# New orders of issue in a four-mixer block kernel: opening loads, mLSTM heads with a mask table, input blocks, merges and boundaries turned by pairs

## What is computed

```python
h = x
u = rmsnorm(h, norm_mix[0]); h = h + mlstm_mixer(u, ...)     # stage A: 4 heads, 128 wide keys, 256 wide values
h = h + swiglu(rmsnorm(h, norm_ffn[0]), w_in[0], w_out[0])   # hidden width 2816
u = rmsnorm(h, norm_mix[1]); h = h + moba_mixer(u, ...)      # stage B: 8 heads of 128
h = h + swiglu(rmsnorm(h, norm_ffn[1]), w_in[1], w_out[1])
# stage C, the second network's block
p = rms_norm(h, norm1) @ w_in_2                              # window attention, hyena, differential attention, 3 gates
a = window_attention(...)        # 8 query heads of 64, masked to a distance of 128
b = hyena_branch(...)            # short convolution, two long convolutions by spectra of generated filters, gates
c = diff_attention(...)          # 4 heads, two softmaxes subtracted, then an rms norm
merged = sigmoid(g0) * (a @ w_oa) + sigmoid(g1) * (b @ w_ob) + sigmoid(g2) * (c @ w_oc)
h = h + merged @ w_out_2
out = h + swiglu(rms_norm(h, norm2), ...)
```

## Time and profile before

| | us |
|---|---|
| median of 3 runs | 1113.66 |
| lowest, highest | 1113.09, 1119.86 |
| profiled execution, its own time | 1115.49 |
| its span, first to last instruction | 1113.7 |
| TensorE busy in it | 1072.1 |
| VectorE, ScalarE busy | 722.5, 539.7 |

### The profile page before, as it was taken

The page is one execution under the profiler, slowest core; times in us unless marked ns, Lnnn a source line. Parts: engine busy times, 40 slices in busy tenths (PEclk is TensorE's granted clock), DMA queues, the critical chain, the costliest instruction groups (busy, mean ns, idle before and its releaser), DMA issues.

```text
span 1113.7 us, 14635 instructions
## 1 busy us (share of the span) xinstructions
PE 1072.1 (96%) x4942; PEld 865.8 (78%) x4942; DVE 722.5 (65%) x1209; ACT 539.7 (48%) x828; POOL 40.0 (4%) x48
## 2 busy tenths in 40 slices
PE   5999999999999999999999999899999999999998
PEld 3777678888887778788888878676777777888887
DVE  2865876555557987754554579787868666555553
ACT  3564355443444546643443464446456445443442
POOL 5003000000000200000000000000000000000000
PEclk9999999999999999999999999999999999999999
DMA  9464256655565544566555553543444355655553
GB/s 256 123 169 132 77 153 193 191 188 183 189 189 170 169 151 126 158 189 186 189 188 181 179 170 97 168 132 114 136 146 133 118 182 163 190 188 182 189 188 112
DMA packets 133598, 182.04 MB, mean 163 GB/s; under 512 B 11446, under 2 KB 80322, under 8 KB 133490
## 3 DMA queue, kind: packets, MB, share of 16 engines
q1 hardware_dynamic: 132266, 178.40, 50.9%
q0 software_dynamic: 1056, 2.57, 1.1%
q10 hardware_dynamic: 232, 0.49, 0.1%
HBM read 180.36 MB, written 1.05 MB: 163 GB/s over the span
## 4 chain that ended last, share of the span: by engine, by line
PE 76%; DVE 14%; ACT 5%; issue 2%; DMA 1%; SPq 1%; POOL 0%; DVEq 0%; ACTq 0%; POOLq 0%
PE ps L1802 15%; PE ps L1813 14%; PE ps L1805 14%; PE ps L1823 7%; PE ps L1824 7%; PE ps L1828 7%; DVE wlo L998 4%; PE ps L1787 2%; PE ps L1789 2%; PE ps L1788 2%; PE ps L1893 1%; DMA raw<-in_a_w_in 1%; ACT whi L537 1%; PE ps L1876 1%; PE ps L2015 1%
## 5 line engine op out<-in xcount | busy, mean ns | idle before, releaser
L998 DVE TENSOR_TENSOR wlo<-raw,whi 128x1024 fp32r<-128x1024 f32 x338 | 406.6, 1234 | 145.3 <-ACT whi L537 144.7
L537 ACT ACTIVATE whi<-raw 128x1024 fp32r<-128x1024 f32 x338 | 342.3, 1052 | 117.7 <-DMA raw<-in_ffn_w 27.6
L1802 PE MATMUL ps<-whi,ath 128*128 128x512 f32 (+1 forms) x896 | 359.3, 402 | 8.3 <-DVE atl L1012 4.3
L1805 PE MATMUL ps<-whi,atl 128*128 128x512 f32 (+1 forms) x896 | 351.4, 393 | 0.0
L1813 PE MATMUL ps<-wlo,ath 128*128 128x512 f32 (+1 forms) x896 | 241.4, 391 | 3.3 <-DVE wlo L998 3.3
L1802 PEld LDWEIGHTS ps<-whi,ath 128*128 128x128 f32 x896 | 169.6, 189 | 52.6 <-issue 12.0
L1813 PEld LDWEIGHTS ps<-wlo,ath 128*128 128x128 f32 x896 | 168.0, 189 | 40.3 <-DVE wlo L998 5.3
L1805 PEld LDWEIGHTS ps<-whi,atl 128*128 128x128 f32 x896 | 169.8, 189 | 33.3 <-issue 0.5
L1823 PE MATMUL ps<-whi,brh 128*128 128x512 f32 x272 | 106.5, 392 | 0.4 <-issue 0.4
L1824 PE MATMUL ps<-whi,brl 128*128 128x512 f32 x272 | 105.9, 389 | 0.0
L1074 DVE TENSOR_TENSOR brl<-ps,brh 128x512 fp32r<-128x512 f32 x33 | 22.8, 692 | 94.6 <-ACT brh L583 94.6
(11 more groups left out here) (339 smaller groups left out, 1006.5 us busy)
## 6 DMA issues: line engine op xcount, KB each, us to landing
raw<-in_ffn_w_in SPq DMA_DIRECT2D x176, 256.0 KB, 2.9
raw<-in_ffn_w SPq DMA_DIRECT2D x132, 256.0 KB, 2.9
raw<-in_w_in SPq DMA_DIRECT2D x104, 256.0 KB, 2.9
raw<-in_ffn_w_out SPq DMA_DIRECT2D x88, 256.0 KB, 2.8
raw<-in_a_w_in SPq DMA_DIRECT2D x48, 256.0 KB, 3.3
raw<-in_b_w_in SPq DMA_DIRECT2D x48, 256.0 KB, 3.0
raw<-in_a_w_out SPq DMA_DIRECT2D x16, 256.0 KB, 2.8
raw<-in_b_w_out SPq DMA_DIRECT2D x16, 256.0 KB, 2.8
```

The costliest lines, as they stand in the source:

```text
L537: a_(unit_view(whi, slot, w), unit_view(raw, slot, w), ACT.Copy).then_inc(hi_ready, 1)
L998: v_.tensor_tensor(unit_view(wlo, slot, w), unit_view(raw, slot, w), unit_view(whi, slot, w), ALU.subtract).then_inc(lo_ready, 1)
L1802: mm(ps[bk + t][:, 0:w], ath[:, k, t * P:(t + 1) * P], rh[:, kk, :], start=k == 0, stop=False)
L1805: mm(ps[bk + t][:, 0:w], atl[:, k, t * P:(t + 1) * P], rh[:, kk, :], start=False, stop=False)
```

## The change

No arithmetic changes but the mask of stage A: a table `maskA` of 128x256 (large values above the diagonal, then zeros) takes the place of the constant 0.0 in `a_dist`'s max, so that exp gives zero there, and GpSimd's `affine_select` goes. The rest moves instructions.

```diff
 # opening, SyncE: x first, unit 0, small rows, units on
-nc.sync.dma_start(con[:, 0:P], D["consts"][:, 0:P])
-sp.wait_ge(sem("cleared"), 1)
-nc.sync.dma_start(grow[0:mix.shape[0], :], mix)
 for t in range(NT):
     nc.sync.dma_start(x[:, t, :], xv[:, t, :])
+load_in(U_A, D["a_w_in"][0], 0)
+sp.wait_ge(sem("cleared"), 2)
 for name, src, w in rows: ...
-for i in range(6):
+for i in range(1, 6):
     load_in(U_A + 4 * i, D["a_w_in"][0], 512 * i)
 # GpSimd: the two small filter weights first, then in steps
+nc.gpsimd.dma_start(fw12[0:33, 0, :], ...)
+nc.gpsimd.dma_start(fw12[:, 1, :], ...)
+pool.wait_ge(raw_loaded[0], 32)
 nc.gpsimd.dma_start(wg[:, :, :], ...)
 ... # the twelve parameters
+pool.wait_ge(raw_loaded[1], 64)
+pool.wait_ge(sem("filt_loaded"), 32)
 nc.gpsimd.dma_start(A_dec, D["decay"])
 nc.gpsimd.dma_start(work[0:64, 18968:18968 + 2048], D["filt_w3_2"][0])
-for h in range(AH):
-    pool.wait_ge(sem("a_p_ready"), h + 1)
-    ... nc.gpsimd.affine_select(out=blk, in_=blk, ...)
 # ScalarE
-nc.scalar.dma_start(con[:, P:N_FIRST], ...)
+nc.scalar.dma_start(con[:, 0:P], ...)
+nc.scalar.dma_start(grow[0:mix.shape[0], :], mix)
+turn_hi(0, mix_gain, (0,))
 feed(1)
-turn_hi(0, ...)
+nc.scalar.dma_start(con[:, P:N_FIRST], ...)
+turn_hi(0, mix_gain, (1, 2, 3))
 # TensorE: five products of zeros, x turned tile by tile of tokens, the small rows' transpose and
 # the filter product behind block 0 and in block 1
+pe.wait_ge(sem("cleared"), 1)
+for _ in range(5):
+    mm(ps[7][:, 0:S], hid[:, 0, 0:P], hid[:, 0, :], start=True, stop=True)
-turn(lambda t: x[:, t, :], x_first)
+for t in range(NT):
+    pe.wait_ge(sem(f"x_loaded{t}"), 16)
+    for p in range(4): ... transposes of tile t
+units(0, use=0)
 nc.tensor.transpose(ps[7][:, 256:384], grow[:, :], ident)
-units(0, use=0)
-units(1, beside=gate_products)
+units(1, 0, 2, beside=gate_products)
+mm(ps[7][0:64, 0:S], fw12[0:33, 0, :], ...)
+units(1, 2, 4, beside=gate_products)
 # stage A's heads
-feed(24 + AHEAD)                      # ScalarE and VectorE, ahead of the heads
+dve.wait_ge(sem("con2_loaded"), 64)
-v_.tensor_scalar(A_D[...], mb[:, 0:S], am[:, 0, h:h + 1], 0.0, ALU.subtract, ALU.max)
+v_.scalar_tensor_tensor(A_D[...], mb[:, 0:S], am[:, 0, h:h + 1], maskA, ALU.subtract, ALU.max)
-pe.wait_ge(sem("a_p_masked"), 2 * h + 2)
+pe.wait_ge(sem("a_p_ready"), h + 1)
+evac(5, ...)                          # now ahead of a_weights(2)
-norm_sum(1)                           # VectorE: now behind turn_lo(1, (0, 1)) and spectrum(2)
 # boundaries, five places
-down_end(end, ..., at=(1, 1), between=lambda: x_turn(r + 1, (0, 1)))
+down_end(end, ..., between={(1, 0): turn pair 0, (1, 1): turn pair 1})
 # stage C: window blocks ahead of the hyena's third part
-C_COLS = ((768, 512), (1280, 512), (1792, 512), (0, 512), (512, 256), (2304, 512), ...)
+C_COLS = ((768, 512), (1280, 512), (0, 512), (512, 256), (1792, 512), (2304, 512), ...)
 # TensorE
-units(15, 0, 1); backward(0); units(15, 1, 3); h_back(1); units(15, 3, 4); forward(1); units(16)
+units(15, 0, 2); backward(0); units(15, 2, 4); units(16, 0, 1); h_back(1); units(16, 1, 2); forward(1); units(16, 2, 4)
 # VectorE, behind hyena_gate(0)
-feed(20); spectral(1); feed(21); spectral_imag(1); feed(22); spectral_end(1); feed(24)
-c_sums x3; h_taps(2); feed(26); c_norms; rotations of both token tiles
+feed(18); c_sums x3; c_norms; c_rotate(0, 0, 8, 0, None)
+feed(20); spectral(1); feed(22); spectral_imag(1); feed(24); spectral_end(1); feed(25); h_taps(2); feed(26)
+the other rotations
 # ScalarE, ahead of the window heads
+a_(sm[:, 126:127], con[:, 0:1], ACT.Exp)          # ahead of the wait for c_w_turned
-act.wait_ge(sem("h_z"), 4); a_(obh[...], h_v, ACT.Copy)   # now behind w_exp(0) and its splits
+w_exp(0) ahead of feed(W_STEPS[0]); c_squares of C_pd behind w_pt(0)
 # VectorE: w_logits(0) ahead of feed(U_C + 32), w_prob(0) behind it
 # differential heads and merges
-feed(D_STEPS[0]); merge(0, ...)
+feed(U_GC + 2); merge(0, ...); feed(D_STEPS[0])
-d_exp(2) whole; gate_evac(24, 0)
+d_exp(2, comp 0); gate_evac(24, 0); d_exp(2, comp 1)
+down_unit(U_OB, ...)                  # TensorE: ahead of d_pv(3)
-one rsqrt and scaling for four heads; feed(U_OC + 2) ahead of c_hi and c_lo
+d_norms(0), d_norms(1) by two heads, each with its own transposes; feed(U_OC + 3) ahead of c_hi and c_lo
-merge(1, both halves); feed(U_W + 2); merge(2, half 0); turn_lo(6, (0, 1)); merge(2, half 1)
+merge(1, half 0); merge(1, half 1, tile 0); merge(2, half 0); feed(U_W + 2); turn_lo(6, (0, 1))
+feed(U_W + 3); merge(1, half 1, tile 1); merge(2, half 1)
-mg_turn((0, 1)) at (3, 0) of the U_OC down_end; down_unit(U_W); mg_turn((2, 3)); units 1 to 5 of U_W
+mg_turn((0, 1)) at (2, 1); down_end of units 0 to 2 of U_W; mg_turn((2, 3)); units 3 to 5
```

More of the change, by code:

```diff
@@ L104 @@
 _at = 0
-for _name, _n in (("ident", P), ("ones", P), ("sel", AH * P), ("zT", S), ("nrmw", 4), ("inv", BROT // 2),
+for _name, _n in (("ident", P), ("ones", P), ("sel", AH * P), ("zT", S), ("nrmw", 4), ("inv", BROT // 2), ("maskA", S),
                   ("cosC", NT * HD // 2), ("sinC", NT * HD // 2), ("maskB", 384), ("maskW", NT * S),
@@ L799, in h_evac @@
             def h_evac(c):
-                evac(12 + c, lambda t: C_ph[:, c, t, :], n=4, tiles=(0, 1))
+                evac(H_BLOCKS[c], lambda t: C_ph[:, c, t, :], n=4, tiles=(0, 1))
             def h_conv(c):
@@ L1683, in _, with merge @@
             feed(U_OA + 4)
-            def merge(b, banks, u_last, halves=(0, 1)):
+            def merge(b, banks, u_last, halves=(0, 1), tiles=range(NT)):
                 gate = (C_th2, C_th, C_th2)[b]
@@ L1693, in merge @@
                         dve.wait_ge(unit_used, u_last)
-                    for t in range(NT):
+                    for t in tiles:
                         th = gate[:, t, nb * 512:(nb + 1) * 512]
@@ L1751, in _ @@
                 feed(D_STEPS[min(i, CH)])
[L1753 to L1761 removed]
+            d_norms(0)
+            d_norms(1)
+            feed(U_OC + 3)
             for p in range(2):
@@ L1843, in down_end @@
                         for t in range(NT):
-                            if nb and (i, t) == at:
-                                between()
+                            if nb and between and (i, t) in between:
+                                between[i, t]()
                             ins = split_mm(ps[banks[2 * nb + t]][:, :], acts[0][:, k, t * P:(t + 1) * P],
@@ L1943, in ffn @@
                 if r < 4:
-                    down_end(end, (brh, brl), at=(1, 1), between=lambda: x_turn(r + 1, (0, 1)))
+                    down_end(end, (brh, brl), between=by_pairs(lambda p: x_turn(r + 1, p)))
                 else:
                     down_end(end, (brh, brl))
+            pe.wait_ge(sem("cleared"), 1)
+            for _ in range(5):
+                mm(ps[7][:, 0:S], hid[:, 0, 0:P], hid[:, 0, :], start=True, stop=True)
             pe.wait_ge(sem("ident_loaded"), 16)
@@ L1952, in _ @@
             nc.tensor.transpose(ps[6][:, 0:16], grow[0:16, :], con[0:16, 0:16]).then_inc(sem("cols_turned"), 1)
-            def x_first(p):
-                if p == 0:
-                    for t in range(NT):
-                        pe.wait_ge(sem(f"x_loaded{t}"), 16)
-            turn(lambda t: x[:, t, :], x_first)
+            for t in range(NT):
+                pe.wait_ge(sem(f"x_loaded{t}"), 16)
+                for p in range(4):
+                    for f in range(2):
+                        c = (2 * p + f) * P
+                        ins = nc.tensor.transpose(ps[TBANKS[p]][:, f * S + t * P:f * S + (t + 1) * P],
+                                                  x[:, t, c:c + P], ident)
+                    if t == NT - 1:
+                        ins.then_inc(turned, 1)
+            units(0, use=0)
             pe.wait_ge(sem("grow_loaded"), 16 * (len(GROWS) - 1))
@@ L2427, in _ @@
                         d_scores(h + 2)
+                if h == CH:
+                    pe.wait_ge(sem("h_lo"), 1)
+                    pe.wait_ge(sem("d_exp"), 4 * CH)
+                    down_unit(U_OB % RING, 0, True, False, U_OB + 1, obh, obl, OB_BANKS)
                 if h >= 1:
                     d_pv(h - 1)
-            pe.wait_ge(sem("h_lo"), 1)
-            pe.wait_ge(sem("d_exp"), 4 * CH)
-            for k in range(3):
-                down_unit((U_OB + k) % RING, k, k == 0, False, U_OB + k + 1, obh, obl, OB_BANKS)
             for p in range(2):
-                if p == 0:
-                    pe.wait_ge(sem("d_y"), 2)
+                k = p + 1
+                down_unit((U_OB + k) % RING, k, False, False, U_OB + k + 1, obh, obl, OB_BANKS)
+                pe.wait_ge(sem("d_y"), 2 * p + 2)
                 for f in range(2):
```

254 lines of the change are left out of this document (142 added, 112 removed).

## The result

| | before | after |
|---|---|---|
| median | 1113.38 | 1088.64 |
| lowest, highest | 1112.41, 1119.86 | 1085.49, 1089.00 |
| profiled execution, its own time | 1115.49 | 1089.00 |
| its span | 1113.7 | 1087.1 |

The ratio is 0.975, with a 95% interval from 0.9721 to 0.9778: 24.7 us less, where 28.7 were forecast. The time lies inside the range, 0.6 above the interval of the forecast case (1080 to 1088).

The account below looks back on a forecast made before the run. TensorE bounds the kernel, busy 1072.1 of 1113.7 us, so only idle time and half clock can be won. Terms sum to 29.0: 1086.5 from the profiled 1115.5, 1084.7 against the median, said as 1085; range 1079 to 1098.

Parts of the forecast that it names:

- Rival 1: Opening stays bound by loads and gives 4.5 us less: 1089 to 1090; chance 0.17.
- Rival 2: VectorE really bounds stage C, removed waits return behind the next split: about 1095 us; chance 0.17.
- Rival 4: Slower: fillers leave TensorE's clock at half level for long, some 1127 us; chance 0.02.
- The opening: Kernel start to end of block 0: earlier first product and shorter block 0, 9.1 us (4.5 to 10.9).
- the 1.0 for late loads: In block 0: 1.0 us added because units 1 to 3 share DMA with constants and parameters.
- no half-clock stretch after the opening: Sign of being right: TensorE is granted no stretch at half clock once the opening is over.
- the sign that I gave for block 1: Sign of being wrong: splits of 2 us and more beside GpSimd in block 1, TensorE waiting at them.
- Stage A's heads: Three TensorE waits in stage A, at the mask, second spectrum and L1823, shrink: 3.1 us (0.8 to 3.4).
- Boundaries: Turning x by pairs gains 0.5 us at each of four boundaries, nothing at the first: 2.0 (lower bound -1.2).
- Second hyena round: Sums, norms and largest rotation move into VectorE's idle time, removing the 2.7 wait at L1813: 5.0 us (1.5 to 5.7).
- First window head: ScalarE's table load goes into idle time, three operations behind the exp, removing a 1.7 wait: 3.6 us (1.5 to 3.8).
- Differential heads and merges: Stage C waits at scores, gate evacuation, d_pv(3) and merges shrink through reordering: 6.2 us (3.0 to 6.9).

Follow-up runs that it names:

- e6: Kernel of e1 with VectorE's list around the hyena's second spectrum as before, the blocks' new order kept: 1085.8 us.
- e12: Kernel of e1 with VectorE's merges in their old order, TensorE's list staying new: 1086.43 us.
- e1: Changed kernel with one wait more: GpSimd's sum and difference of the filters' third weights wait until VectorE has the gate logits: 1081.2 us.
- e11: Kernel of e1 with stage A's mask applied by GpSimd's affine_select again and 0.0 in place of the table: 1083.41 us.
- e5: Kernel of e1 with boundaries turned in one go again, all four column tiles of x ahead of the last three products: 1082.75 us.
- e7: Kernel of e1 with ScalarE's list ahead of the first window head as before (table load, copy into obh and splits together): 1084.67 us.
- e10: Changed kernel with GpSimd's two table loads swapped, ScalarE's roundings of units 8 and 9 ahead of the sine, gate logits behind one split: 1081.09 us.
- e2: Changed kernel with the first filter product behind the first unit of block 1 instead of the second: 1081.26 us.
- e8: Kernel before with the new opening alone (loads, fillers, x by tiles, filter product in block 1, GpSimd's queue): 1109.78 us.
- e9: Changed kernel with GpSimd's two table loads swapped, so the filters' third weights land earlier; order of the lists unchanged: 1088.18 us.
- e4: Changed kernel without the five filler products of the opening: 1088.03 us.

## Why the prediction was right, and where its steps failed

**The bound held.** No product went away, and what was won is idle time of TensorE and half clock. Rival 1, an opening that stays bound by loads, fell at the first product (9.48). That the measured 1088.64 lies beside its 1089 to 1090, nearer than to my 1085, is luck: its mechanism didn't happen. Rival 2, VectorE as the real bound of stage C, fell with the missing waits from 660 to 830. It was true in one respect: e6 and e12 show that in stage C VectorE's order is worth 4.6 and 5.2 us. The order was the limit, not VectorE's work, which is 67% of the span. Rival 4 needed the clock low for over 58 us and it was low for 10.

**The opening, 9.1 forecast, 3.1 in the end.** Up to the end of block 0 the forecast was too low: 11.0, just above its upper bound of 10.9. I had put SyncE's nine small issues between unit 0 and unit 1, but `load_in` issues all four units of a block, and the timeline has them from 1.67 to 6.03, the small rows behind. So the 1.0 for late loads wasn't needed, and block 0 took 11.4 instead of 12.4. The first product came at 9.48 instead of 10.4. No run undoes the load order by itself, so how the 11.0 divide between loads, turning x by tiles and the moved GpSimd work isn't shown.

The step that failed is the one about GpSimd's operations: "VectorE is units ahead, and 3.0 lost by it are hidden. If that cover is gone they cost up to 3." The cover is counted in units split ahead, but what was slowed was no split. It was the filter's argument, a chain with no units in it, on which ScalarE's roundings hung by order alone. In units ScalarE was ahead when it reached the sine, and it lost that lead standing there for 10.75 us. And the price was more than 3: a wait of 4.05 and 3.8 of half clock behind it, of which e1 gives back 7.4. My number stayed within 4 us of the measured one because the rest of the sum came out higher, and that part is luck. No rival of mine described the wait, and of my signs "no half-clock stretch after the opening" failed, while the sign that I gave for block 1, splits of 2 us and more, didn't show: its three splits took 3.50.

I had quoted the right warning and set it aside. By the Trainium skill, SBUF — State Buffer, section Who interferes with whom, a VectorE instruction with two SBUF inputs contends with a GpSimd instruction that reads SBUF, so the collision was moved and not removed. The trace agrees, with 4.2 lost on VectorE (2.60 and 2.48 against twice 0.42), where I had reckoned 3.0.

**Stage A's heads, 3.1 forecast, 3.6 measured** between 95 and 138. The 1.4 for the mask measured 1.6 in e11. The wait for `atl` at the next output product went from 1.3 to 0.5, near the 1.0 that I took off.

**Boundaries, 2.0 forecast, 1.5 measured (e5).** That nothing would be won in the first held: 0.80 of wait for the residual there. The 0.5 at each of the others measured somewhat less: the two waits of 0.9 became 0.2, but in two other places a wait for the residual and the switches take back part.

**Second hyena round, 5.0 forecast**, 5.7 between the traces, 4.6 by e6. **First window head, 3.6 forecast**, 5.1 between the traces, 3.5 by e7. **Differential heads and merges, 6.2 forecast**, 7.9 between the traces with the fifth boundary in it; e12 alone gives 5.2. In each the mechanism was the one named, and the waits came back with the size of the earlier trace rows when the order was undone. The undo runs give less than the traces' differences. One reason is that each puts back only one engine's list. The clock may be another: I had counted 1.7 for a half-clock stretch behind each of the three waits. The kernel before has these stretches; the profiled executions of e6, e7 and e12 have the waits back and not the stretches. The executions without a trace needn't be so: their mean clock is 0.999 to 1.000 in e6, but 0.998 in three of e7 and in two of e12, which leaves room for one stretch of 3.4 us each (an estimate), so the medians don't tell what the stretches cost.

The sum of the forecast was 29.0 against 26.6 between the traces: 6.0 too much for the opening, 3.6 too little for the rest.

## What to carry to other kernels

When an operation is moved next to a chain, count the cover in what the chain's followers need, not in how many units of bulk work an engine is ahead: a queue that issues in order turns one slow small operation into idle time for everything behind it. Put bulk work that is already loaded ahead of the wait for such a chain, as e10 does; then the chain's end holds up only what needs the chain itself. And read a gain at the next places downstream as well: 11.0 us were in hand at 20.9 and 3.1 at 53.9, and an experiment that changes the lead ahead of such a wait (the fillers) shows nothing in the time.

## What the runs showed of the hardware

- Beside GpSimd's two `TENSOR_TENSOR` operations not only VectorE's operations with several inputs are held up. In e10 two `TENSOR_SCALAR` of 64x256 on one tile in SBUF took 1.69 and 2.35, where they take 0.28 alone; the one ahead of them, which reads PSUM and started 0.25 after GpSimd, kept its 0.54. Each of these short operations ends within 0.3 of the end of the GpSimd operation beside it. The splits of 1.2 in e2 end 1.1 behind it (37.80 and 41.11, against 36.7 and 40.03). Both look like an operation that is held until GpSimd's ends and then runs for its own length. In proportion short operations lose most: 0.28 became 2.35, and a split of 1.2 became 1.90 or 2.78. The Trainium skill, SBUF — State Buffer, section Who interferes with whom, says that `tensor_scalar` can enter the modes that take the shared pair of ports as well, and that whoever issues second is fully blocked for the whole of the other's instruction; the trace agrees.
- The collision goes both ways: GpSimd's two operations took 4.75 in e10, and 5.74 in e1 and 5.69 in e2, where a split of VectorE had started before one of them.
- The same wait of 4.0 us was followed by 10.24 us at half clock in the changed kernel and by 3.4 in e8; waits of 3.1 (e9) and 3.0 (e4) by 10.3 and 6.8. Waits of 2.25 (e12), 1.7 (e7) and two of 1.3 (e6) were followed by none in their profiled executions, where the kernel before has a stretch of 3.4 behind waits of 2.2, 1.7 and 2.7. A half-clock stretch behind a wait of that size is a risk and not a price.
- The landing of the filters' third weights moved by over two microseconds between traces of kernels that issue the load at the same place (GpSimd starts on them at 31.64 in the changed kernel, at 34.06 in e4 and at 34.34 in e2). What such a load releases on GpSimd falls beside different work each time, so an order that holds for only one of the two is fast by luck.
- The granted clock of the first microseconds doesn't fit the lengths. The profile gives 1.00 for 0 to 10 in the changed kernel, yet its ten filler instructions of 256 columns take 0.46 each there, where products of 257 columns follow each other every 0.22 at 100 us. So x's transposes at 3.65 (before), 3.50 (e4) and 2.13 (changed) tell more of the clock there than the column, which the earlier trace rows has at 1.00 over them too.
